# Pool linear of two channel groups as three split products in a hybrid decoder step

## What is computed

```python
def multiscale_pool(u_full, first_pos, n_ctx, w_pool, pool_scale):
    ...
    for g, win in enumerate(POOL_WINDOWS):          # windows 2, 4, 8, 16: one per group of 512 channels
        ...
        mean = (cs[:, j + 1, sl] - cs[:, lo, sl]) / cnt[None, :, None]
        d = mean - uf[:, n_ctx:, sl]
        outs.append(jnp.einsum('btc,cd->btd', d, w_pool[g].astype(F32)))
    return (jnp.concatenate(outs, axis=-1) * pool_scale.astype(F32)).astype(u_full.dtype)

mix = jnp.concatenate([o_a * jax.nn.silu(g_a), o_b * jax.nn.silu(g_b)], axis=-1)
h = x + jnp.einsum('btm,md->btd', mix, w_out)
```

## Time and profile before

| | |
|---|---|
| median of 3 runs | 2042.63 us (2040.45 to 2045.72) |
| profiled execution, its own time | 2044.04 us |
| its span, first to last instruction | 2042.4 us |
| PE busy | 99% of the span |
| DVE, ACT, POOL busy | 67%, 35%, 22% |
| granted PE clock, mean | 0.997 |

### The profile page before, as it was taken

How to read it: one execution, slowest core, us unless ns; L and a number is a source line. 1 busy time by engine, 2 the same in 40 slices (tenths; PEclk the granted TensorE clock), 3 DMA queues, 4 the chain that set the end, 5 groups by cost and what they waited for, 6 DMA issues and landing times. The chain is left out here.

```text
span 2042.4 us, 37259 instructions
## 1 busy us (share of the span) xinstructions
PE 2025.1 (99%) x13401; PEld 1920.6 (94%) x13401; DVE 1360.7 (67%) x1974; ACT 719.3 (35%) x885; POOL 456.7 (22%) x675
## 2 busy tenths in 40 slices
PE   9999999999999999999999999999999999999998
PEld 7888888899999999999999999999999999999997
DVE  5787777887777545566767776756565856665565
ACT  7434333322222333333332233333334433333333
POOL 2222212122221020045643002121213411111100
PEclk9999999999999999999999999999999999999999
DMA  8899989866655565656666557798888755555554
GB/s 239 278 313 304 309 296 303 285 201 174 184 160 162 174 193 169 184 171 198 182 209 195 174 172 233 211 295 273 270 276 282 239 166 169 165 165 169 155 161 150
DMA packets 315674, 439.51 MB, mean 215 GB/s; under 512 B 21324, under 2 KB 251660, under 8 KB 313288
## 3 DMA queue, kind: packets, MB, share of 16 engines
q1 hardware_dynamic: 260936, 291.75, 47.6%
q0 software_dynamic: 37168, 128.17, 19.0%
q10 hardware_dynamic: 17488, 18.55, 2.7%
HBM read 394.31 MB, written 48.22 MB: 217 GB/s over the span
## 5 line engine op out<-in xcount | busy, mean ns | idle before, releaser
L288 PE MATMUL main<-XX,hi 128*128 128x320 f32 x3264 | 1029.7, 315 | 0.2 <-DVE lo L258 0.2
L290 PE MATMUL main<-XX,lo 128*128 128x320 f32 x3264 | 1009.1, 309 | 0.0
L289 PE MATMUL main<-XX,hi 128*128 128x320 f32 x3264 | 1008.8, 309 | 0.0
L258 DVE TENSOR_TENSOR lo<-raw,hi 128x1024 fp32r<-128x1024 f32 x542 | 686.1, 1268 | 442.8 <-ACT hi L253 440.0
L253 ACT ACTIVATE hi<-raw 128x1024 fp32r<-128x1024 f32 x542 | 570.0, 1057 | 864.2 <-PE main L290 529.1
L288 PEld LDWEIGHTS main<-XX,hi 128*128 128x128 f32 x3264 | 613.6, 188 | 7.0 <-issue 2.0
L289 PEld LDWEIGHTS main<-XX,hi 128*128 128x128 f32 x3264 | 613.6, 188 | 2.6
L290 PEld LDWEIGHTS main<-XX,lo 128*128 128x128 f32 x3264 | 613.2, 188 | 0.0
L272 PE MATMUL main<-hi,XX 128*128 128x512 f32 x512 | 199.4, 389 | 0.0
L273 PE MATMUL main<-hi,XX 128*128 128x512 f32 x512 | 199.2, 389 | 0.0
L274 PE MATMUL main<-lo,XX 128*128 128x512 f32 x512 | 199.2, 389 | 0.0
(11 more groups left out here) (310 smaller groups left out, 1623.9 us busy)
## 6 DMA issues: line engine op xcount, KB each, us to landing
raw<-w_in SPq DMA_DIRECT2D x416, 512.0 KB, 4.4
raw<-w_out SPq DMA_DIRECT2D x128, 512.0 KB, 3.7
kin<-cache_k POOLq DMA_DIRECT2D x64, 256.0 KB, 5.8
turnedK<-kout POOLq DMA_DIRECT2D x64, 256.0 KB, 6.1
deck<-turnedK POOLq DMA_DIRECT2D x8, 2048.0 KB, 8.8
projT<-stg ACTq DMA_DIRECT2D x35, 320.0 KB, 3.2
keep<-cache_v POOLq DMA_DIRECT2D x40, 256.0 KB, 3.5
deck<-cache_v POOLq DMA_DIRECT2D x24, 256.0 KB, 4.1
```

What stands on the lines that cost most here:

```text
L258: nc.vector.tensor_tensor(low, raw[:, slot, :, 0:width], high.bitcast(F32), ALU.subtract).then_inc(lo_ready, 1)
L288: nc.tensor.matmul(sums, wh, XH[:, k, :], start=first, stop=False)
L289: nc.tensor.matmul(sums, wh, XL[:, k, :], start=False, stop=False)
L290: mm = nc.tensor.matmul(sums, wl, XH[:, k, :], start=False, stop=last)
```

## The change

- The pool linear of quads 1 and 2 (channel groups 1 and 2) no longer uses plain float32 matmuls. ACT rounds the rows `dl` and the weights `wp` of the group into `dlH` and `wpH` (fp32r), DVE writes the rests into `dlL` and `wpL`, and each plain matmul becomes three. Quads 0 and 3 stay as they are.
- In those two quads the four places of the pool linear move from j = 3, 7, 11, 15 to j = 7, 8, 11, 15. ACT splits at j = 4, ahead of `pT`, and DVE at j = 5 and 6, behind the chunk's `lo`.
- The four new buffers take the place of `ubuf` and of quad 0's `dl`. So ACT's first split waits until group 3's `poolT` is stored (`u_st` 16 * NG). Rows of groups 1 to 3 go to a part of `stT` (the transposed pooling state, named `keep` in the rows), and so does the gate's `ex` from quad 1 on, while quad 0 keeps its old place. Therefore `group_load(1)` also waits for `gated_b` 7, the third gate step of the second half of quad 0.

```diff
@@ -465,9 +465,9 @@
...
+         u_in, u_step, u_st, w_in_, w_pe, w_ev, w_hi, w_lo) = (sem(n) for n in (
+             "a_st", "ts_step", "ts_fin", "u_in", "u_step", "u_st", "w_in_", "w_pe", "w_ev", "w_hi", "w_lo"))
@@ -1224,17 +1224,26 @@
             tops = sb("tops", [N_S, 8], ctx=ph)
             cntr = sb("cntr", [P, NG, STATE + 1], ctx=ph)
             fix = sb("fix", [P, 4, STATE + 1], ctx=ph)
+            with ExitStack() as early:
+                ubuf = [sb(f"ubuf{i}", [P, 4, UW], ctx=early) for i in range(3)]
+                dl0 = sb("dl0", [P, 4, N], ctx=early)
+            dlH, dlL = (sb(n, [P, 4, N], F32R, ctx=ph) for n in ("dlH", "dlL"))
+            wpH, wpL = (sb(n, [P, 4, 4 * P], F32R, ctx=ph) for n in ("wpH", "wpL"))
+            sb("gap", [P, 128], ctx=ph)
             obuf = sb("obuf", [P, 4, N], ctx=ph)
-            ubuf = [sb(f"ubuf{i}", [P, 4, UW], ctx=ph) for i in range(3)]
             uin = sb("uin", [P, 4, N], ctx=ph)
-            dl = sb("dl", [P, 4, N], ctx=ph)
             wp = sb("wp", [P, 4, 4 * P], ctx=ph)
+            WHOLE = {3: 0, 7: 1, 11: 2, 15: 3}
+            SPLIT = {7: 0, 8: 1, 11: 2, 15: 3}
             uflat = uin[:].rearrange("p a n -> p (a n)")
             ut = uflat[:, 0:4 * P].rearrange("p (a n) -> p a n", a=4)
             utN = uflat[:, 4 * P:8 * P]
 
             old = (POOLW // P - 4) * NB_S * STATE
-            gex = stT.rearrange("p a n -> p (a n)")[:, old - 2 * N:old].rearrange("p (a n) -> p a n", a=2)
+            states = stT.rearrange("p a n -> p (a n)")
+            gex = [states[:, a:a + 2 * N].rearrange("p (a n) -> p a n", a=2) for a in (old - 2 * N, 4 * N)]
+            assert 6 * N <= POOLW // P * NB_S * STATE
+            dl = [dl0[:], states[:, 0:4 * N].rearrange("p (a n) -> p a n", a=4)]
             NQ = segs["u"][2]
             HPQ = H // (2 * NQ)
             ROUNDS = TOPK_S // 8
@@ -1365,17 +1374,19 @@
                         head_load(pool, 1, 0, 0)
                     head_store(pool, 0, q, 1)
 
-                def group_load(q):
+                def group_load(q, split=1):
                     pool.wait_ge(w_pe, q * 4)
+                    if split:
+                        pool.wait_ge(gated_b, 7)
                     pool.wait_ge(u_st, q * 16 + 16)
                     alone(pool)
                     pool.dma_start(wp[:], t["w_pool"][0, ds(q, 1)].rearrange("g (a p) d -> p (g a) d", p=P)).then_inc(w_in_, 16)
-                    pool.dma_start(dl[:], tiles(poolT, q * 4, 4)).then_inc(w_in_, 16)
+                    pool.dma_start(dl[split], tiles(poolT, q * 4, 4)).then_inc(w_in_, 16)
 
                 def turn_load(q):
                     pool.dma_start(ut, projT[ds(q * 4 + T_U, 4), :, N - P:N].rearrange("a p n -> p a n")).then_inc(ut_in, 16)
 
-                group_load(0)
+                group_load(0, 0)
                 group = pool_steps(pool, NQ - 1)
                 next(group)
                 turn_load(0)
@@ -1407,7 +1418,10 @@
                         turn_load(q + 1)
                         head_load(pool, 1, q + 1, 1)
 
-            def pe_weave(half):
+            def pe_weave(half, split=False, end=False):
+                at_ = SPLIT if split else WHOLE
+                rows = dl[int(end)]
+
                 def weave(pe, q, j):
                     u, s = j // 8, j % 8
                     g = 2 * half + u
@@ -1434,16 +1448,23 @@
                         nc.tensor.matmul(sbank[2][:, P:T_P], vN[:, 0, gv], pT[:, P:2 * P], start=True, stop=False)
                         nc.tensor.matmul(sbank[2][:, P:T_P], vN[:, 1, gv], pT[:, 2 * P:L2], start=False,
                                          stop=True).then_inc(a_pv, 1)
-                    if half and j % 4 == 3:
-                        dt = j // 4
-                        if dt == 0:
-                            pe.wait_ge(w_in_, q * 32 + 32)
+                    if half and j in at_:
+                        dt = at_[j]
+                        if dt == 0 and split:
+                            pe.wait_ge(w_lo, q * 2)
+                        elif dt == 0:
+                            pe.wait_ge(w_in_, 32 * (q + 1))
                         pe.wait_ge(w_ev, q * 4 + dt)
                         if dt == 3:
                             pe.wait_ge(ut_c, q + 1)
                         for a in range(4):
-                            mm = nc.tensor.matmul(sbank[3][:, 0:N], wp[:, a, dt * P:(dt + 1) * P], dl[:, a, :],
-                                                  start=a == 0, stop=a == 3)
+                            cols = slice(dt * P, (dt + 1) * P)
+                            if not split:
+                                mm = nc.tensor.matmul(sbank[3][:, 0:N], wp[:, a, cols], rows[:, a, :], start=a == 0, stop=a == 3)
+                                continue
+                            nc.tensor.matmul(sbank[3][:, 0:N], wpH[:, a, cols], dlH[:, a, :], start=a == 0, stop=False)
+                            nc.tensor.matmul(sbank[3][:, 0:N], wpH[:, a, cols], dlL[:, a, :], start=False, stop=False)
+                            mm = nc.tensor.matmul(sbank[3][:, 0:N], wpL[:, a, cols], dlH[:, a, :], start=False, stop=a == 3)
                         mm.then_inc(w_pe, 1)
                     if half and j == 13:
                         pe.wait_ge(ut_in, q * 16 + 16)
@@ -1453,9 +1474,16 @@
                         tr.then_inc(ut_t, 1)
                 return weave
 
-            def act_weave(half, last=False):
+            def act_weave(half, last=False, split=False):
                 def weave(act, q, j):
                     u, s = j // 8, j % 8
+                    if split and j == 4:
+                        act.wait_ge(w_in_, q * 32 + 32)
+                        act.wait_ge(w_pe, q * 4)
+                        act.wait_ge(u_st, 16 * NG)
+                        act.wait_ge(w_pe, 4)
+                        nc.scalar.activation(dlH[:], dl[1], ACT.Copy).then_inc(w_hi, 1)
+                        nc.scalar.activation(wpH[:], wp[:], ACT.Copy).then_inc(w_hi, 1)
                     n = q * HPQ + (half * NQ * HPQ + u)
                     if s == 2:
                         act.wait_ge(a_mx, n + 1)
@@ -1475,9 +1503,17 @@
                             act.dma_start(qS, projT[T_Q:T_Q + H, :, T_P:N].rearrange("h p n -> p h n")).then_inc(e_in, 16)
                 return weave
 
-            def dve_weave(half, last=False):
+            def dve_weave(half, last=False, split=False):
+                at_ = SPLIT if split else WHOLE
+
                 def weave(dve, q, j):
                     u, s = j // 8, j % 8
+                    if split and j == 5:
+                        dve.wait_ge(w_hi, q * 2 - 1)
+                        nc.vector.tensor_tensor(dlL[:], dl[1], dlH[:].bitcast(F32), ALU.subtract).then_inc(w_lo, 1)
+                    if split and j == 6:
+                        dve.wait_ge(w_hi, q * 2)
+                        nc.vector.tensor_tensor(wpL[:], wp[:], wpH[:].bitcast(F32), ALU.subtract).then_inc(w_lo, 1)
                     n = q * HPQ + (half * NQ * HPQ + u)
                     if s == 0:
                         dve.wait_ge(a_rel, n * 32 + 32)
@@ -1527,24 +1563,29 @@
 
             def on_scalar(act):
                 act_segment(act, "u", act_weave(0))
-                gate = (gex, exped_b, gated_b, 4, (obuf, w_ev))
+                first_gate, gate = ((x, exped_b, gated_b, 4, (obuf, w_ev)) for x in gex)
                 act.wait_ge(u_st, 16 * (NG - 1))
-                with act.Fori(0, NQ - 1) as q:
-                    act_quad(act, "gb", q, act_weave(1), gate=gate)
+                act_quad(act, "gb", 0, act_weave(1), gate=first_gate)
+                with act.Fori(1, NQ - 1) as q:
+                    act_quad(act, "gb", q, act_weave(1, split=True), gate=gate)
                 act_quad(act, "gb", NQ - 1, act_weave(1, True), gate=gate)
 
             def on_vector(dve):
                 dve.wait_ge(d_in, 48 + 16 * NB_S)
                 nc.vector.tensor_tensor(scS[:, PAST:LS], scS[:, PAST:LS], negS[:], ALU.add).then_inc(ts_step, 1)
                 dve_segment(dve, "u", dve_weave(0))
-                gate = (gex, exped_b, gated_b, 4, (obuf, w_ev))
-                with dve.Fori(0, NQ - 1) as q:
-                    dve_quad(dve, "gb", q, dve_weave(1), gate=gate)
+                first_gate, gate = ((x, exped_b, gated_b, 4, (obuf, w_ev)) for x in gex)
+                dve_quad(dve, "gb", 0, dve_weave(1), gate=first_gate)
+                with dve.Fori(1, NQ - 1) as q:
+                    dve_quad(dve, "gb", q, dve_weave(1, split=True), gate=gate)
                 dve_quad(dve, "gb", NQ - 1, dve_weave(1, True), gate=gate)
 
             def on_tensor(pe):
                 pe_segment(pe, "u", pe_weave(0))
-                pe_segment(pe, "gb", pe_weave(1))
+                pe_quad(pe, "gb", 0, pe_weave(1))
+                with pe.Fori(1, NQ - 1) as q:
+                    pe_quad(pe, "gb", q, pe_weave(1, True))
```

(5 more changed lines are left out.)

## The result

The changed kernel takes 2052.95 us (2050.14 to 2053.83, 6 runs) against 2042.98 (2040.45 to 2046.15, 6 runs) in the same job. The ratio is 1.0042, 95% interval 1.0031 to 1.0052, so by the ratio it is slower by some 8.6 us; the two medians themselves lie 10.0 us apart. The span of its profile is 2051.9 us, 9.5 more than before.

What follows compares the result with a forecast made beforehand. PE, busy 99%, was taken as the bound. Gain -3.1, first wait +4.8 and second wait +2.8 made +4.5 us on 2042.63, so 2047.1 us; the range was 2042.5 to 2052.0 us.

Steps and rivals of the forecast that it cites:

- the case that had 0.38: Whole kernel: slower than before by over 0.3% (6.1 us); chance 0.38.
- a landing of 8.6 us: Group 3's `poolT` store in quad 1 landing in 8.6 instead of 5.2 us, adding 3.4 us.
- rival 1: Start of quad 1: POOL and DVE block each other, store 3.0 us later, net +7.5 us; chance 0.38 with milder forms.
- The gain: Split groups in quads 1 and 2: 1.76 instead of 2.15 us each, saving 3.1 us in all.
- Quad 2: Split copies there finish before PE needs them, 1.7 us of cover left, so no cost.
- The first wait: Quad 1: ACT waits for group 3's store, delaying `pT` and PE's value product by 4.8 us.
- The bound 1.6: Extra store lateness in quad 1, 1.6 us, at which the slowdown reaches 6.1 us, or 0.3%.
- The second wait: Quad 1, end of chunk 7: PE stands 2.8 us for `wpL` from DVE.

Runs made afterwards that it cites:

- plain products: Changed kernel with all its splits and waits kept, but PE multiplies the unsplit operands in plain matmuls; ratio 1.0049 to the kernel before.
- all three orders: Changed kernel with POOL's group 3 store before its gate wait, ACT's copies behind `pT`, DVE's two subtractions at j = 4; ratio 0.9992 to the kernel before.
- DVE first: Changed kernel with both of DVE's split subtractions at j = 4, ahead of the `lo` of chunk 8; ratio 1.0028 to the kernel before.

## Why the prediction was right, and where it was not

The forecast was +4.5 us; it is +8.6 by the ratio of the times and +8.0 by D. The sign and the place were right, the size was half. It is 0.42% slower, outside the 0.3% to which the prediction gave 0.58, and so the case that had 0.38. The range reached up to 2052.0 us. By the ratio the changed kernel comes to 2042.63 x 1.0042 = 2051.2, inside; by the two medians, 10.0 apart, it would be 2052.6, just outside. That it fell inside is in part luck: the upper end was made of a landing of 8.6 us and half of rival 1. The landing took 5.4, and what came in its place, the fall of the clock, was in no term.

- **The gain.** Forecast 3.1 us. The runs agree: 0.39 us a group from the plain products in quad 2, and the run with all three orders. By the rule of the Trainium skill, page "FP8 and Floating Point Precision", section "TensorE Precision Notes", that a true float32 product is four passes, it would have been 4.3; the measurement does not agree, and it decides.
- **Quad 2.** Covered, as forecast: `wpL` ends at 1204.1, PE starts the first group at 1206.68, so 2.6 us of cover were left. (The prediction wrote 1.7, where its own numbers, 1197 and 1195.6, give 1.4.) Only 0.3 us were lost, where PE, without the linear group at j = 3, came to its transposes just before `lg` was ready. I had not looked at that.
- **The first wait.** Forecast 4.8, measured 6.3: the value product started at 1130.63, and without a wait it would have at 1126.53 - 2.15 - 0.05 = 1124.33, the last term because quad 1 began 0.05 earlier. The copies had the lengths forecast (1.27 and 1.90), but ACT came free at 1127.1, not 1125.5. The step that failed is the price of the `lo` inside the scaling pass: I took 1.75 us by the earlier trace rows, it took 4.37 and ended at 1111.67. From its start to the end of `lg` it was 1.9 us more than forecast; it began 0.5 earlier than forecast, so `lg`, the bias load and the store came 1.4 us later than forecast. The landing took 0.2 more. This is rival 1 in its place, at half its price: the `lo` started as the scaling pass did, and ended 0.2 before the pass. The bound 1.6 from which it was to decide was not reached by it alone. By the Trainium skill, page "SBUF — State Buffer", section "Who interferes with whom", the instruction that comes second is blocked for as long as the first lasts. The trace shows the direction, not the full length: a `lo` that begins beside the pass ends about when the pass does, with no 1.2 us of its own behind it., where the `lo` began 2.7 us into the pass and took 1.75, fit that reading as well; I had read them as a small price, and they may as well have been the tail of the same block.
- **The second wait.** Forecast 2.8, measured 2.7, and removed by the order of DVE alone.
- **The clock.** Not in the forecast, and the term that was missing: the forecast put what a wait does to the clock at nothing, without a reason. Behind the second wait PE ran 14 distances in 3.58 us, from 1138.64 to 1142.22, instead of 14 x 0.1465 = 2.05: 1.5 us more. The first fall, at 1121.6, was covered by the wait for `pT`, and so was PE's 2.3 us for `lg`.

The sum by these is 6.3 + 2.7 + 1.5 + 0.3 - 3.1 = 7.7, of 8.0.

**Open:** six of the eleven profiles have PE waiting 1.5 us for a `lo` in the output stage, at about 1600 us (from the last linear group to the end it is 741.4 there, else 739.8). In the profile before it isn't there, in the changed kernel it is, twice; but two changed versions, measured in another job, don't have it. The traces show what goes with it. Some 20 us ahead of that wait a subtraction of POOL, which starts when a load has landed, and one of DVE start within 0.6 us of one another. In the six profiles with the wait POOL's is first, by 0.0 to 0.3 us, and DVE's takes 3.7 us; in the other five DVE's is first, by 0.06 to 0.6 us, and takes 1.5. In the changed kernel, then before:

```profile
1587.59 2.53 POOL L1767 TENSOR_TENSOR keep<-keep 128x1024 f32<-128x1024 f32 x1 [0.44 <-DMA keep<-projT]
1587.78 3.68 DVE L1874 TENSOR_TENSOR XX<-deck,XX 128x1280 fp32r<-128x1280 f32 x1
```

```profile
1579.94 1.49 DVE L1833 TENSOR_TENSOR XX<-deck,XX 128x1280 fp32r<-128x1280 f32 x1
1580.00 3.71 POOL L1726 TENSOR_TENSOR keep<-keep 128x1024 f32<-128x1024 f32 x1 [0.71 <-DMA keep<-projT]
```

Whether the change has a part in who comes first, I can't say; it was not tried apart. The 1.5 us are in the span and in the times, not in D.

## What to carry to other kernels

When an engine that is never late gets work that waits for another engine's last step, follow that step's own chain first, with everything that a new wait in front of it moves: here a wait of POOL for the gate moved a pass beside the one subtraction on which the matmuls stood. Put such a split behind what others wait for (`pT`), and take its second half at once instead of in turn. A wait of a saturated TensorE should be priced with what the clock may do behind it, here 1.5 us.

## What the runs showed of the hardware

A VectorE subtraction with two SBUF inputs took 1.23 us alone and 4.37 us when it began 0.1 us behind a GpSimd pass of 4.65 us. A wait of 1.8 to 2.6 us on TensorE was followed by 3.4 us at the lower clock in some places and not in others: the wait of 1.9 us at chunk 3 was so in one kernel (DVE first) and not in the changed one, where the wait of 2.2 us for `lg` was, in both profiles, and in the kernel with ACT's copies behind `pT` and DVE first neither of these two waits was. The split products start 0.147 us apart at full clock and 0.267 at the lower, as those of the stream do.
